# RWKV scan: chunk inverse in seven products instead of ten, key products in the other array corners, two VectorE operations moved to GpSimd

## The chip, the cores and the metric

One Trainium2 chip, one core. The metric is device time in microseconds (us) of one execution of the whole program, the median of the runs shown.

## The reference, cut to what matters

The program is a two-part transformer stack. The change touches one stage, the RWKV-7 recurrence, which runs in both directions over 768 tokens (256 of context, 512 of sequence) for 16 heads of 64 channels:

```python
def _wkv_step(S, inp):
    r_t, w_t, k_t, v_t, a_t, b_t = inp
    sa = jnp.einsum('zbhvk,zbhk->zbhv', S, a_t)
    S = S * w_t[..., None, :] + sa[..., :, None] * b_t[..., None, :] + v_t[..., :, None] * k_t[..., None, :]
    return S, jnp.einsum('zbhvk,zbhk->zbhv', S, r_t)
```

The kernel does it in chunks of 64 tokens. Inside a chunk the `sa` rows depend on each other through a strictly triangular 64x64 matrix, so that each chunk needs the inverse R of (1 - that matrix).

## The kernel before, in words

`rwkv_scan` (L3537) treats one head at a time, 12 chunks a head, in 3 groups (NG) of 4 chunks. The forward direction lies on partitions 0 to 63 (`lo`), the backward one on 64 to 127 (`hi`). So each product is two 64x64x64 matmuls, one per direction; `mmul` (L3957) issues both, each in the corner of the array whose rows and output partitions are the same half (lo to lo, hi to hi). `to_rows` (L3966), which adds rows of the result y, sends for odd chunks lo rows to hi partitions and hi rows to lo partitions.

The work of a head h is software-pipelined over three heads. `body` of TensorE (from L4026 on) has, interleaved by hand:

- for head h the *pair products* (`pair_set`, L4056: bh and kh against at_rt; 4 chunks 64 wide, 8 chunks 128 wide) and the *turns* (`turn`, L4068: bh and kh times a diagonal, 64 wide, 11 chunks); VectorE masks the pairs (`mask`, L3869), scales them (`scale`, L3881), makes R of the first level (`add_eye`) and its transpose T;
- for head h the *inverse*: five doubling levels (LEVELS = 5) of 3 groups, NZ = 15 steps, each of two products: `grow_z` (off x T, L4099), copied to Z by ScalarE (`copy_z`, L3792), and Z x R, added to R by VectorE (L3941), which then transposes R to T again (L3895). GpSimd makes the 15 masked `off` tiles (L3708) and the first R (L3703);
- for head h-1 the *walk*: 12 chunks j, each a chain of three parts, `walk_state` (X), `walk_solve` (SA = R X) and `walk_share` (state Sm). ScalarE copies X, SA and Sm out of PSUM (L3727, L3731, L3736), and the next part's matmul waits for that copy. The parts of chunks 0 to 2 and the first of chunk 3 lie among pair products and turns; the other 26 lie one by one in the 30 slots of the inverse (WALK_PARTS, L3545);
- for head h+1 the *factors*, spread over the same slots: five 128x768 activations on ScalarE, 14 operations on VectorE (`factor_part`, L3824), three on GpSimd (`factors`, L3682: km, kh, eed).

Every engine works through its own list in order, so a wait holds all that stands behind it. In VectorE's list, after `add_eye`, stand `add_bonus` (L3911), `split_block` (L3926: w_lo = w_raw - w_hi, 128x512) and `add_shift` (L3920: the bias, 128x256); the inverse's additions come after these. The DMA queue (SP) stores w_hi and w_lo once w_lo is made, loads the next block once the bias is added, and then loads factors and v of later heads.

The walk of the last head (15) runs in the next stage, `walk_finish` (L4188), beside the output projection.

## Time and profile before

| | |
|---|---|
| median of 3 runs | 4038.56 us (4037.82 to 4040.61) |
| span of the profiled execution | 4039.7 us, from its first to its last instruction |
| the scan in it | from 2812.16 us (first pair product of head 0) to about 3399 us |
| mean granted TensorE clock | 0.970 of full speed |

The profiled execution is known by its span alone; it lies 1.1 us over the median of the runs, inside their spread. A PE row is a matmul: each fp32 product of one direction is two records, so one `mmul` is x4. A row `x2` or `x4` merges records that follow each other. The duration of a PE row is from issue to the end of its results; what a product costs in a dense stretch is the step from one row's start to the next. PEclk is the granted clock (1.00 is 2.4 GHz, 0.50 is 1.2 GHz). A row of busy time by stretch gives start and end, length, then busy time and count of PE, PEld (weight loads), DVE (VectorE), ACT (ScalarE) and POOL (GpSimd), PEclk, the DMA share and GB/s. In square brackets at a row's end stands the idle time before it and what ended it.

### The profile page before, as it was taken

To read this page: it belongs to the slowest core of one execution; us is meant where nothing else is said; L and a number is where in the kernel's file an instruction comes from. 1 tells how busy PE (TensorE), PEld (TensorE's weight loads), DVE (VectorE), ACT (ScalarE), POOL (GpSimd) and SP (SyncE) were. 2 spreads that over 40 slices of the span, in tenths; PEclk is the share of its full clock that TensorE was granted. 3 is DMA by queue.
4 is the path that set the end of the run, shared out by engine and by line. 5 is a ranking of instruction groups with operands and counts; after the bars stand their busy time and mean duration, and the time that the engine had idled before them with its cause. 6 is when DMAs were issued, how large, how long until landed. Compare 5 with 4: busy or idle time off the path is not lost. (4 is left out here: it accounts for less than half of the span.)

```text
span 4039.7 us, 81581 instructions
## 1 busy us (share of the span) xinstructions
PE 3727.0 (92%) x32706; PEld 2683.2 (66%) x32706; DVE 2360.8 (58%) x3864; ACT 1204.0 (30%) x2668; POOL 1321.7 (33%) x1020
## 2 busy tenths in 40 slices
PE   8888999898999999899999997998999999899887
PEld 6667878657787898777344444874999998733333
DVE  4568882545985445565444445767888776623333
ACT  3352222344222322331111112224455454111112
POOL 4443444434445364573000000431555453000000
PEclk9999999999999999999999999999999999899999
DMA  4114542303554122345999995356333234589997
GB/s 128 56 53 170 184 157 93 104 1 105 178 187 146 66 96 75 99 138 228 404 420 420 420 420 212 134 177 201 88 89 91 78 93 147 199 366 422 421 421 316
DMA packets 231204, 787.80 MB, mean 195 GB/s; under 512 B 56008, under 2 KB 64024, under 8 KB 171136
## 3 DMA queue, kind: packets, MB, share of 16 engines
q1 hardware_dynamic: 225008, 764.12, 50.9%
q0 software_dynamic: 5328, 19.40, 1.2%
q8 instruction: 219, 3.59, 0.4%
q14 instruction: 73, 0.60, 0.0%
q10 hardware_dynamic: 576, 0.09, 0.0%
HBM read 736.15 MB, written 47.38 MB: 194 GB/s over the span
## 5 line engine op out<-in xcount | busy, mean ns | idle before, releaser
L2887 POOL DMA_INDIRECT moe0e_xg<-moe_h,moe_first_rows x20 | 18.9, 947 | 546.3 <-DVE moe_first_rows L3044 540.5
L3011 ACT ACT_TABLE_LOAD x32 | 41.1, 1283 | 519.2 <-PE moe1e_p_u L2957 262.4
L373 POOL TENSOR_TENSOR gmi_w_lo<-gmi_rows_w,gmi_w_hi 128x512 fp32r<-128x512 f32 x64 | 120.2, 1878 | 159.8 <-ACT gmi_w_hi L415 159.8
L3960 PE MATMUL scan_bank<-scan_T,scan_off 64*64 64x64 f32 x3840 | 159.4, 220 | 8.5 <-issue 5.7
L373 POOL TENSOR_TENSOR p_w_lo<-p_rows_w,p_w_hi 128x512 fp32r<-128x512 f32 (+3 forms) x88 | 113.5, 1291 | 159.9 <-ACT p_w_hi L415 159.9
L2887 POOL DMA_INDIRECT moe1e_xg<-moe_h,moe_first_rows x17 | 16.0, 940 | 451.0 <-DVE moe_first_rows L3044 444.4
L1159 POOL TENSOR_TENSOR f0u_w_lo<-f0u_w,f0u_w_hi 128x1024 fp32r<-128x1024 f32 x42 | 115.0, 2757 | 137.6 <-ACT f0u_w_hi L1175 137.6
L1159 POOL TENSOR_TENSOR f1u_w_lo<-f1u_w,f1u_w_hi 128x1024 fp32r<-128x1024 f32 x42 | 114.3, 2742 | 137.5 <-ACT f1u_w_hi L1175 137.5
L1227 DVE SCALAR_TENSOR_TENSOR f0u_ada<-hT,condition,f0u_ada 128x512 f32<-128x512 f32 x168 | 148.2, 949 | 16.4 <-DMA hT<-in_ada_w_dram 15.9
L1227 DVE SCALAR_TENSOR_TENSOR f1u_ada<-hT,condition,f1u_ada 128x512 f32<-128x512 f32 x168 | 140.5, 903 | 20.5 <-DMA hT<-in_ada_w_dram 20.0
L2984 PE MATMUL moe0e_p_y<-moe_ring,moe0e_gatedT 128*64 128x512 f32 x608 | 137.6, 605 | 7.8 <-ACT moe0e_gatedT L3013 7.8
L3960 PEld LDWEIGHTS scan_bank<-scan_T,scan_off 64*64 64x64 f32 x3840 | 137.2, 135 | 10.5 <-issue 6.8
L373 POOL TENSOR_TENSOR rp_w_lo<-rp_rows_w,rp_w_hi 128x512 fp32r<-128x512 f32 x48 | 79.9, 1666 | 164.8 <-ACT rp_w_hi L415 164.8
L2984 PE MATMUL moe1e_p_y<-moe_ring,moe1e_gatedT 128*64 128x512 f32 x512 | 113.4, 595 | 10.8 <-DVE x L3040 9.4
L3797 ACT ACTIVATE scan_Z<-scan_bank 128x256 f32<-128x256 f32 x240 | 91.4, 381 | 97.1 <-PE scan_bank L3960 95.8
L3960 PE MATMUL scan_bank<-walk_memory 64*64 64x64 f32 x1708 | 116.0, 222 | 4.3 <-issue 1.7
L2957 PE MATMUL moe0e_p_g<-gm_uT,moe0e_xT 128*64 128x512 f32 x444 | 118.1, 600 | 0.8 <-ACT moe0e_xT L3005 0.8
L2957 PE MATMUL moe0e_p_u<-gm_uT,moe0e_xT 128*64 128x512 f32 x444 | 116.2, 592 | 0.0
L440 DVE CAST gmi_x_hi<-hT 128x768 fp32r<-128x768 f32 x64 | 42.9, 670 | 125.2 <-PE gmi_bank L362 124.9
L2984 PEld LDWEIGHTS moe0e_p_y<-moe_ring,moe0e_gatedT 128*64 128x64 f32 x608 | 50.0, 139 | 86.8 <-issue 71.3
L3708 POOL TENSOR_TENSOR scan_off<-scan_pairs,scan_join 128x256 f32<-128x256 f32 x120 | 101.3, 880 | 0.0
L3708 POOL TENSOR_TENSOR scan_off<-walk_memory,scan_join 128x256 f32<-128x256 f32 x120 | 100.4, 873 | 0.0
(903 smaller groups left out, 11529.7 us busy)
## 6 DMA issues: line engine op xcount, KB each, us to landing
moe_ring<-in_moe_w_down_dram SPq DMA_DIRECT2D x140, 1024.0 KB, 18.0
gm_uT<-in_moe_w_gu_dram SPq DMA_DIRECT2D x111, 1024.0 KB, 16.6
moe_ring<-in_moe_w_gu_dram SPq DMA_DIRECT2D x102, 1024.0 KB, 24.7
walk_memory<-in_moe_w_gu_dram SPq DMA_DIRECT2D x60, 1024.0 KB, 24.4
hT<-in_ada_w_dram SPq DMA_DIRECT2D x48, 1024.0 KB, 6.8
f0u_w<-in_ffn_w_gate_up_dram SPq DMA_DIRECT2D x22, 1024.0 KB, 4.8
f1u_w<-in_ffn_w_gate_up_dram SPq DMA_DIRECT2D x22, 1024.0 KB, 4.8
gmi_rows_w<-in_ga_w_in_dram SPq DMA_DIRECT2D x64, 256.0 KB, 2.7
```

Of the source, the lines that this page charges most:

```text
L373: nc.gpsimd.tensor_tensor(w_lo[t % 2][:, 0:width], w[t % RAW][:, 0:width], w_hi[t % 2][:, 0:width], ALU.subtract).then_inc(w_lo_made, 1)
L440: nc.vector.tensor_copy(x_hi[t % 2][:, tok], hT[:, k, tok]).then_inc(x_hi_made, 1)
L1159: nc.gpsimd.tensor_tensor(w_lo[u][:, g], w[:, g], w_hi[u][:, g], ALU.subtract).then_inc(lo_made, 1)
L1227: ins = V.scalar_tensor_tensor(out=acc[:, z, :], in0=src, scalar=cond[:, n * HALF + k, z:z + 1], in1=acc[:, z, :], op0=ALU.mult, op1=ALU.add)
L2887: pool.indirect_dma_start(xg[:], None, H.h, bass.IndirectOffsetOnAxis(rows[:, 0:1], 0)).then_inc(gathered, 16)
L2957: mm = nc.tensor.matmul(p[r, :], xT[:, kd, r], weights(s, half, second)[:, k, g * HID:(g + 1) * HID], start=(kd == 0), stop=(kd == KD - 1) ...
L2984: mm = nc.tensor.matmul(p_y[n][r, :], aT[:, kh, r], ring[s, half][:, k, n * BANK:(n + 1) * BANK], start=(kh == 0), stop=(kh == KH - 1), sk ...
L3011: nc.scalar.activation(sg[:], p_g[:], ACT.Silu).then_inc(silu_ready, 1)
L3708: nc.gpsimd.tensor_tensor(off[n][:], strict(u, g), over4(join[:, l + 1, :]), ALU.mult).then_inc(s["off_ready"], 1)
L3797: A(Z[n % 2][:], quad(z_bank[n % 2]), ACT.Copy).then_inc(s["z_copied"], 1)
L3960: mm = nc.tensor.matmul(out[r], lhsT[r], rhs[r], start=start, stop=stop, skip_group_check=True)
```

## The change

The inverse takes 7 products per group instead of 10: with blocks of 32 (BLOCK_BITS) W is the part of the matrix inside the blocks beyond the first level; a first product gives the power (FIRST), three products Z x [power, R] of 128 columns square the power and extend R at once (stages 1 to 3), one adds the last power, and two (OUTER, FINAL) join the two blocks of 32. They are issued in 30 UNITS, the 9 squaring products in two halves. ScalarE copies the power (`copy_power`), VectorE adds and transposes. All products with kh (pairs, turns) and those of the walk with v use the other two corners of the array (`crossed`: hi rows to lo partitions and the reverse); v is loaded with its halves swapped, and pairs of b and of k get PSUM banks and masks of their own. The products with v move ahead of the part that needs them. `split_block` and `add_shift` go from VectorE's list to GpSimd's, right behind the masks. In `walk_finish` the walk gets the same order.

```diff
-LEVELS = 5
+BLOCK_BITS = 5
+PRODUCTS = 7
...
-                    for z, rows in ((0, lo), (1, hi)):
+                    for z, rows in ((0, hi), (1, lo)):
...
+                def split_block(h):
+                    pool.wait_ge(s["hi_made"], h + 1)
+                    nc.gpsimd.tensor_tensor(w_lo[:], w_raw[:], w_hi[:], ALU.subtract).then_inc(s["lo_made"], 1)
+
+                def add_shift(h):
+                    hs = slice(h * HK, h * HK + HK)
+                    pool.wait_ge(s["bonus_done"], h + 1)
...
                 def body(h, walk, ahead):
                     u = h % 2
+                    if h:
+                        pool.wait_ge(s["r_added"], h * ADDED)
                     for g in range(NG):
...
-                    for n in range(NZ):
-                        l, g = n // NG, n % NG
-                        if h:
-                            pool.wait_ge(s["z_ready"], (h - 1) * NZ + n + 1)
-                        nc.gpsimd.tensor_tensor(off[n][:], strict(u, g), over4(join[:, l + 1, :]), ALU.mult).then_inc(s["off_ready"], 1)
+                        nc.gpsimd.tensor_tensor(WR[:, g4, 1, :], strict(u, g), over4(join[:, 0, :]), ALU.mult).then_inc(s["r_joined"], 1)
+                        nc.gpsimd.tensor_tensor(off[:, g4, :], strict(u, g), over4(join[:, 1, :]), ALU.mult).then_inc(s["off_ready"], 1)
+                    for g in range(NG):
+                        nc.gpsimd.tensor_tensor(off_outer[:, 4 * g:4 * g + 4, :], strict(u, g), over4(join[:, 2, :]), ALU.mult).then_inc(s["outer_ready"], 1)
+                    split_block(h)
+                    add_shift(h)
                     if ahead is not None:
                         factors(ahead)
...
+                    copy_turned(0)
+                    early_walk(walk_sm, 1)
...
                     copy_turned(1)
+                    early_walk(walk_x, 2)
+                    early_walk(walk_sa, 2)
                     copy_turned(2)
+                    early_walk(walk_sm, 2)
+                    early_walk(walk_x, NG)
...
+                    def copy_power(n):
+                        act.wait_ge(s["r_added"], h * ADDED + adds_through(n))
+                        A(WR[:, chunks(n), 0, :], both(n)[:, :, 0, :], ACT.Copy).then_inc(s["z_copied"], 1)
+
+                    for k, (n, (first, end)) in enumerate(UNITS):
+                        if n // NG in (FIRST, OUTER):
+                            copy_z(n)
+                        walk_part(walk, k - 1)
+                        if squares(n) and end == 4:
+                            copy_power(n)
+                        if ahead is not None and k % 2 == 0 and k:
+                            factor_part(ahead, k // 2 - 1)
...
-                    mask(0)
+                    mask_b(0)
                     scale(0)
-                    mask(1)
-                    mask(2)
+                    mask_k(0)
+                    mask_b(1)
                     scale(1)
-                    mask(3)
-                    mask(4)
+                    add_eye(0)
+                    mask_b(2)
                     scale(2)
-                    add_eye(0)
+                    mask_k(1)
                     add_eye(1)
+                    mask_k(2)
                     add_eye(2)
...
+                def crossed(out, lhsT, rhs, start=True, stop=True):
+
+                    for r, o in ((hi, lo), (lo, hi)):
+                        mm = nc.tensor.matmul(out[o], lhsT[r], rhs[r], start=start, stop=stop, skip_group_check=True)
                     return mm
...
                     def turn(g):
...
+                        if g == 1:
+                            pe.wait_ge(s["kpairs_masked"], h * NG + 2)
+                            pe.wait_ge(s["bpairs_masked"], h * NG + 3)
...
+                            j, o = 4 * g + q, slice(q * CH, (q + 1) * CH)
+                            mm_b = mmul(banks[:, TURN_BANKS[g], o][:, 0, :], bh[:, j, :], eed[h % 3][:, j, :])
+                            mm_k = crossed(banks[:, TURN_BANKS[g], o][:, 1, :], kh[:, j, :], eed[h % 3][:, j, :])
...
+                            if stage == FIRST:
+                                mm = mmul(one(n)[:, q, :], off[:, j, :], T[:, j, :])
+                            elif squares(n):
+                                mm = mmul(both(n)[:, q], Z[:, j, :], WR[:, j])
+                            elif stage == OUTER:
+                                mm = mmul(one(n)[:, q, :], off_outer[:, j, :], T[:, j, :])
+                            else:
+                                mm = mmul(one(n)[:, q, :], Z[:, j, :], WR[:, j, 1, :])
...
+                    for k, (n, (first, end)) in enumerate(UNITS):
+                        product(n, first, end)
+                        walk_part(k - 1)
```

## Rows read from the trace of the kernel before

**Rows 1.** Busy time by stretch: head 0, heads 1 to 14, head 15.
```profile
2812.16:2847.34 35.18, 30.00 (x752) 28.71 (x754) 29.56 (x63) 12.14 (x24) 21.34 (x22) 0.87 0.48 126
2847.34:3364.48 517.14, 496.11 (x15519) 478.02 (x15516) 417.03 (x841) 267.87 (x840) 280.31 (x294) 1.00 0.31 83
3364.48:3399.27 34.79, 33.38 (x1059) 32.44 (x1054) 22.89 (x47) 15.57 (x56) 13.96 (x18) 1.00 0.11 31
```
**Rows 2.** The same for head 5: up to its first inverse product, and from there on.
```profile
2995.77:3005.98 10.21, 10.21 (x295) 10.18 (x293) 8.44 (x17) 4.12 (x13) 4.95 (x7) 1.00 0.21 42
3005.98:3032.59 26.61, 25.25 (x827) 23.99 (x824) 21.47 (x44) 15.10 (x48) 15.06 (x15) 1.00 0.36 104
```
**Rows 3.** PE in order of time, head 5: 128-wide pairs; first and fifth turn.
```profile
2997.04 0.41 PE L3960 MATMUL scan_bank<-scan_at_rt,scan_kh 64*64 64x128 f32 x4
2997.26 0.41 PE L3960 MATMUL scan_bank<-scan_at_rt,scan_bh 64*64 64x128 f32 x4
...
3002.88 0.31 PE L3975 MATMUL scan_bank<-scan_eed,scan_kh 64*64 64x64 f32 x4
...
3003.35 0.31 PE L3975 MATMUL scan_bank<-scan_eed,scan_kh 64*64 64x64 f32 x4
```
**Rows 4.** PE in order of time, head 5: solve of an odd chunk with its `to_rows`.
```profile
3011.82 0.27 PE L3960 MATMUL scan_bank<-walk_memory,scan_R 64*64 64x64 f32 x2
3011.84 0.27 PE L3969 MATMUL scan_bank<-walk_memory,scan_at_rt 64*64 64x64 f32 x2
...
3011.99 0.27 PE L3960 MATMUL scan_bank<-scan_T,scan_off 64*64 64x64 f32 x2
```
**Rows 5.** The same for the next, even chunk.
```profile
3015.08 0.33 PE L3960 MATMUL scan_bank<-walk_memory,scan_R 64*64 64x64 f32 x4 [0.18 <-ACT walk_memory L3727]
3015.24 0.49 PE L3969 MATMUL scan_bank<-walk_memory,scan_at_rt 64*64 64x64 f32 x4
3015.47 0.38 PE L3969 MATMUL scan_bank<-scan_v,scan_pairs 64*64 64x64 f32 x4
```
**Rows 6.** VectorE by line and shape, heads 1 to 14: busy us, mean ns.
```profile
L3895 DVE STREAM_TRANSPOSE scan_T<-scan_R 128x256 f32<-128x256 f32 x105 | 46.8, 445 | 3.6
...
L3941 DVE TENSOR_TENSOR scan_R<-scan_R,scan_bank 128x256 f32<-128x256 f32 x107 | 44.5, 416 | 33.7 <-PE scan_bank L3960 32.2
...
L3878 DVE TENSOR_TENSOR scan_pairs<-scan_bank,scan_masks 128x512 f32<-128x512 f32 x28 | 19.3, 690 | 5.1 <-PE scan_bank L3960 5.1
```
**Rows 7.** VectorE in order of time, head 5: bonus, weight split, bias.
```profile
3005.11 1.79 DVE L3917 TENSOR_TENSOR rw_y_bonus<-walk_memory,scan_bonus 64x256 f32<-64x256 f32 x2
3006.93 1.10 DVE L3928 TENSOR_TENSOR scan_w_lo<-scan_w_raw,scan_w_hi 128x512 fp32r<-128x512 f32 x1
3007.96 0.95 DVE L3923 TENSOR_TENSOR rw_y_bonus<-rw_y_bonus,scan_shift 128x256 f32<-128x256 f32 x1
```
**Rows 8.** ScalarE by line and shape, heads 1 to 14: copies of turned keys.
```profile
L3774 ACT ACTIVATE walk_memory<-scan_bank 128x512 f32<-128x512 f32 x14 | 8.4, 598 | 6.1 <-PE scan_bank L3975 6.1
```
**Rows 9.** ScalarE in order of time, head 5: walk copies, a factor.
```profile
3010.34 0.22 ACT L3736 ACTIVATE walk_memory<-scan_bank 128x64 f32<-128x64 f32 x1 [0.43 <-PE scan_bank L3960]
3010.46 0.93 ACT L3749 ACTIVATE scan_sq<-head_memory,head_cols 128x768 f32<-128x768 f32 x1
...
3011.55 0.22 ACT L3727 ACTIVATE walk_memory<-scan_bank 128x64 f32<-128x64 f32 x1
3012.20 0.31 ACT L3731 ACTIVATE walk_memory<-scan_bank,scan_w 128x64 f32<-128x64 f32 x1 [0.43 <-PE scan_bank L3960]
```
**Rows 10.** GpSimd in order of time, head 5: the fifteen masks.
```profile
3003.29 12.67 POOL L3708 TENSOR_TENSOR scan_off<-walk_memory,scan_join 128x256 f32<-128x256 f32 x15
```
**Rows 11.** The page's costliest groups: a weight split on GpSimd, in another stage.
```profile
L373 POOL TENSOR_TENSOR gmi_w_lo<-gmi_rows_w,gmi_w_hi 128x512 fp32r<-128x512 f32 x64 | 120.2, 1878 | 159.8 <-ACT gmi_w_hi L415 159.8
```
**Rows 12.** Busy time by stretch: two successive short stretches of head 0.
```profile
2824.50:2827.90 3.40, 1.17 (x41) 1.03 (x36) 3.33 (x6) 2.11 (x4) 3.40 (x5) 1.00 0.25 91
2827.90:2831.30 3.40, 3.26 (x62) 3.29 (x63) 2.77 (x7) 1.70 (x4) 3.40 (x5) 0.51 0.55 153
```

More of the change, by code:

```diff
@@ L3539, in rwkv_scan @@
     NG = STEPS // 4
-    NZ = LEVELS * NG
+    NI = PRODUCTS * NG
+    ADDED, COPIED, TURNED = 5 * NG, 5 * NG, 6 * NG
+    FIRST, LAST_POWER, OUTER, FINAL = 0, 4, 5, 6
+    UNITS = [(n, part) for n in range(NI) for part in ((0, 4),) * (n // NG not in (1, 2, 3)) + ((0, 2), (2, 4)) * (n // NG in (1, 2, 3))]
+    TURNS_BEFORE = (2, 3, 2, 3)
+    INV_BANK = (2, 1, 3, 0)
     lat = SEQ // CH
@@ L4008, in walk_share @@
+                    if 0 < j < STEPS - 1:
+                        mmul(ds_psum, eed[w % 3][:, j, :], Sm[:], start=False, stop=False)
+                    if i >= 0:
+                        to_rows(i, rt(w, j), Sm[:]).then_inc(s["yr_done"], 1)
                 def walk_share(w, j):
                     u = w % 2
+                    i = j - CSTEPS
+                    if i >= 0:
+                        pe.wait_ge(s["yr_done"], w * lat + i + 1)
                     pe.wait_ge(s["sa_copied"], w * STEPS + j + 1)
@@ L4061, in pair_set @@
                         wide = kinds * CH
[L4062 removed]
+                        for q in range(4):
+                            j, o = 4 * g + q, slice(q * wide, (q + 1) * wide)
                             rhs = at_rt[h % 3][:, 0:kinds, j, :]
[L4064 to L4066 removed]
+                            mm_b = mmul(bank[BPAIR_BANK[g]][:, o], bh[:, j, :], rhs)
+                            mm_k = crossed(bank[KPAIR_BANK[g]][:, o], kh[:, j, :], rhs)
@@ L4129, in _ @@
+                    for k, (n, (first, end)) in enumerate(UNITS):
+                        product(n, first, end)
+                        walk_part(k - 1)
+                        if k == 0:
+                            pe.wait_ge(s["bon_read"], h + 1)
+                        if ahead is not None and k % 2 == 0 and k:
+                            factor_part(ahead, k // 2 - 1)
                 keep_clock(nc, S, bank[7][:, 0:P], 13)
@@ L4148, in rwkv_tables @@
     incl = halves(early | same, early.T | same)
+    strict_of_values, incl_of_values = halves(early.T, early), halves(early.T | same, early | same)
     joins = []
-    for l in range(LEVELS + 1):
+    for l in range(BLOCK_BITS + 1):
         m = 1 << l
@@ L4323, in walk_share @@
                     if j < STEPS - 1:
-                        mmul(ds_psum, walk.bkT[:, j, 0, :], walk.SA[:], start=False).then_inc(ds_ready, 1)
+                        values_to_x(j + 1).then_inc(xv_done, 1)
+                        if i >= -1:
+                            values_to_rows(i + 1, walk.pairs[:, j + 1, 3, :], walk.v[:, j + 1, :], start=i == -1).then_inc(yv_done, 1)
                 def turn_o(t, h):
```

376 lines of the change are left out of this document (196 added, 180 removed).

## The prediction

> **What bounds the kernel now.** I first read busy time by stretch, to see which engine fills the scan. In heads 1 to 14, PE is busy 496 of 517 us at a granted clock of 1.00, 36.94 us a head, while VectorE, the next, is busy 417 us, 29.8 a head [rows 1]. Head 0, which has no walk, is filled by VectorE instead (29.56 of 35.18). In one head, the part before the inverse is solid PE (10.21 of 10.21 us), the rest nearly so (25.25 of 26.61) [rows 2]. So in 15 of 16 heads TensorE's list is the bound. The next question is what a product costs there. In a dense stretch four 64-wide `mmul` take 0.47 us, 0.117 each, and a 128-wide one starts 0.22 after the one before [rows 3].
>
> Then I looked for products in the other corners. `to_rows` of an odd chunk is the only such work beside straight products. There R X and rt Sm start 0.02 us apart, and the next product, 0.17 after the first, finds both issued [rows 4]. For the even chunk, where both use the same corners, the second starts 0.16 after the first and the third 0.23 later: 0.39 for what took 0.17 [rows 5]. So a crossed product beside a straight one is nearly free, for 64 columns at least.
>
> **The change, part by part**, per head. *TensorE's inverse.* Now 30 products of 4 chunks: 120 x 0.117 = 14.0 us. After: 12 products 64 wide, 48 x 0.117 = 5.6, and nine 128 wide, 36 x 0.22 = 7.9: 13.5. That alone gains 0.5.
>
> *Crossed products.* Pairs cost 8 x 0.117 + 16 x 0.22 = 4.5 and turns 22 x 0.117 = 2.6; with every second one beside its neighbour, half: 3.5 gained. In the walk 12 products of v into X and 11 into the state, 23 x 0.117 = 2.7, come to lie beside others. Rows show no 128-wide crossed pair: its gain lies between nothing (as in-line) and all of it; I take all, since the nearest row, rows 4, overlapped fully. Together 6.7 us of PE work go, and 36.9 - 6.7 = 30.2 would be left if TensorE still decided. It will not.
>
> One rule speaks against this. The Trainium skill, "TensorE: Matmul & The Clock Gate" (Part 3), says that a weight load runs beside matmuls in flight only when its row group differs; a crossed product has the row group of a straight one, so by it k would line up behind b. In rows 4 the trace disagrees; by the rule the sum would be that of the rival "no overlap" below.
>
> *What replaces it before the inverse.* I laid out the new lists from the first pair product, T = 0. VectorE's last addition ends at 0.57. A 256-wide mask costs 0.42, like the addition of that shape, a 512-wide one 0.69, a transpose 0.445, scaling and adding the unit 0.42 each [rows 6]. In the new order mask b0 ends at 1.2, k0 2.05, b1 2.8, scale 3.2, the first unit and transpose 4.1, b2 4.8, scale 5.3, k1 6.0, k2 7.6, the last transpose 8.5, the bonus (1.79 [rows 7]) 10.4. TensorE's `turn(1)` has a new wait, for mask k1: it stands from about 4.7 to 6.05, with the walk's chunk 2 queued behind it. ScalarE then copies the turned keys (0.60 [rows 8], about 0.5 for the last group) ahead of X and Sm of chunk 2. That chain (X 7.7, SA 8.4, Sm 9.2) lets the first inverse product go at 9.4 instead of 10.2.
>
> *The 30 units.* 26 walk parts lie among them, one chain. From X's copy to SA's takes 0.65 us at least, ScalarE idle 0.43 of it [rows 9]; SA's copy is 0.09 longer, so the mean link is 0.68. TensorE's work per link is a unit of 0.44 to 0.47, 5.5 straight products per chunk / 3 x 0.117 = 0.21, and 0.05 to restart after a wait (0.16 against 0.117 [rows 5]): 0.73. I take 0.75; 25 links are 18.75. Five factor operations on ScalarE stand in the chain: now Sm to X with one of them and a copy of Z took 1.21 [rows 9], 0.56 over a link; 5 x 0.56 = 2.8. Near the end each product needs its transpose, which VectorE makes only behind the next addition: 2 x 0.42 + 0.445 + 0.3 after a product's end, against a link of 0.75; I count 0.9 for the two places. With 0.5 for the first unit and 0.6 for the last, 0.5 + 18.75 + 2.8 + 0.9 + 0.6 = 23.6. A head takes 9.4 + 23.6 = 33.0, bounds 30.2 (TensorE) and 36.94 (as now): **3.9 less**.
>
> *VectorE.* It loses split and bias (1.10 + 0.95 [rows 7]), gains 3 transposes (1.34) and 0.15 of masks: 29.8 becomes 29.2 of 33.0 us. That is tight, but no bound yet.
>
> *Split and bias on GpSimd.* The split takes 1.88 there [rows 11]; the bias I bound by 0.95 and 1.9. Fifteen masks, 12.67 us [rows 10], become six, and the first R masks stay three: they end near 9.6, the split 11.5, the bias (waiting for the bonus, 10.4) near 12.5 to 13.4. Queued behind are `factors`: km, kh and eed; km started after the old masks, 20.2 us into the head [rows 10], and waits for ScalarE's third factor, near 14. On SP the two stores of the split and the load that waits for the bias go out about where they did (3008.03 and 3008.91 ended, 12.3 and 13.1 into the head [rows 7]); stores and load have the 20 us to the next head's first use. So I cost both at nothing; if that cover were gone, 1.88 + 0.95 = 2.8 a head.
>
> *The sum.* Heads 1 to 14: 14 x 3.9 = 54.6. Head 15 has no factors: 34.79 [rows 1] to 33.0 - 2.8 = 30.2, 4.6. Head 0 is VectorE's: between 0 and 4, I take 2. The last walk keeps its chain: 0, between -1.5 and +1.5. In all 61. The profiled span, 4039.7, is 1.1 over the median, 4038.56; taken from the median: **3978 us**.
>
> **The rivals.** *Better:* links at 0.68 and no loss at the late transposes: 25 x 0.07 + 0.9 = 2.65 a head, 37 in all, 3941. For it: ScalarE's repeated 0.43 idle [rows 9]; against: VectorE at 88%.
>
> *The clock falls.* In head 0 it went to 0.51 after 3.40 us in which PE was busy 1.17 [rows 12]. The wait in `turn(1)` makes such a thin stretch in each head (by my list about 2 of 3.4 us busy). At half clock the 1.3 us of products that follow it (turns, bonus) take twice as long: 14 x 1.3 = 18, so 3996.
>
> *No overlap:* only the 0.5 of the inverse and the gain of heads 0 and 15 at most shrunk likewise: 4038.6 - 15 x 0.5 = 4031. Rows 4 speak against it.
>
> *Slower: the copy of the power holds the walk.* ScalarE's `copy_power` waits for VectorE's addition and stands in front of the next walk copy. VectorE's work apart from masks, scaling, unit, bonus, split, bias, 15 additions and 12 transposes is 29.8 - 22.8 = 7.0 us of factors. If an operation of these stands in front of each of the nine squaring additions (0.77 on average), the walk gets up to 0.77 later nine times. It decides from 3.9 / 9 = 0.43 on; at 0.6 a head gets 5.4 - 3.9 = 1.5 longer: 4038.6 + 21 - 6.6 = 4053. At 0.43 exactly, heads 0 and 15 alone gain: 4032. For it: VectorE's share; against: two links (1.5) hold addition, transpose and 0.63 us more.
>
> **How the numbers follow.** Forecast 0.48 (3978, its own range 3960 to 4000), better 0.14, clock 0.12, no overlap 0.06, the deciding point (4032) 0.07, slower 0.13. A measurement here can tell about 0.2%, 8 us. Faster by more: 0.48 + 0.14 + 0.12 and two thirds of no overlap, 0.78; within: 0.09; slower: 0.13. The range leaves out the slower case and the far tails: 3938 to 4033.
>
> **What would show it.** Right: first pair to first inverse product 9 to 9.8 us, with TensorE idle for VectorE's mask in front of `turn(1)`; pairs of b and k 128 wide starting together, 0.22 per two; heads of 32 to 34 us; PE busy under 85%; the split ending on GpSimd before km without km waiting. Wrong: b and k 0.22 apart each (no overlap); PEclk under 1.00 in heads 1 to 14; ScalarE waiting for VectorE's addition more than 0.4 us per squaring product, or heads over 36 us.

## The result, and the profile after

The changed kernel takes **4068.61 us** (median of 4 runs, 4064.59 to 4069.89), the kernel before 4039.59 beside it: a ratio of 1.0062, with a 95% interval of 1.0049 to 1.0076. The forecast was 3978, the range 3938 to 4033. The change makes the program slower, by 25 us by the ratio and 29 by the medians.

In the profiled execution (span 4067.7) the loss is all in the middle heads. Busy time by stretch, as in [rows 1] and [rows 2]: head 0, heads 1 to 14, head 15 up to its last inverse product, and head 5 in two parts.

```profile
2809.23:2841.02 31.79, 26.66 (x607) 24.04 (x611) 28.14 (x64) 12.03 (x24) 15.40 (x15) 0.84 0.52 140
2841.02:3388.94 547.92, 465.85 (x13510) 422.39 (x13504) 395.89 (x869) 272.08 (x840) 196.66 (x196) 0.93 0.28 78
3388.94:3423.87 34.93, 31.34 (x922) 28.75 (x914) 21.48 (x48) 15.53 (x56) 8.92 (x11) 0.90 0.11 30
...
2994.51:3004.89 10.38, 7.26 (x299) 6.65 (x291) 9.05 (x19) 4.32 (x14) 7.20 (x10) 1.00 0.21 41
3004.89:3032.56 27.67, 24.26 (x685) 21.62 (x682) 19.36 (x44) 15.18 (x47) 6.86 (x5) 1.00 0.33 100
```

Heads 1 to 14 take 547.92 / 14 = 39.14 us instead of 36.94; 14 x 2.2 = 30.8. Head 0 gains 3.4, head 15 loses 1.1 (its last product came 33.83 us into it before). Together +28.5, against 28.0 more of span. TensorE is busy less (465.85 for 496.11), VectorE too (395.89 for 417.03), and yet each head is longer: no engine fills a head now, and the granted clock of the stretch is 0.93, where it was 1.00.

Two things in TensorE's list of head 5, in order of time (columns: start, length, engine, operation; idle time in brackets): products of b and k 128 wide that start together, and a stop in the middle of the first turns.

```profile
2996.17 0.28 PE L4021 MATMUL scan_bank<-scan_at_rt,scan_kh 64*64 64x128 f32 x2
2996.18 0.31 PE L4006 MATMUL scan_bank<-scan_at_rt,scan_bh 64*64 64x128 f32 x2
2996.28 0.28 PE L4021 MATMUL scan_bank<-scan_at_rt,scan_kh 64*64 64x128 f32 x2
2996.29 0.31 PE L4006 MATMUL scan_bank<-scan_at_rt,scan_bh 64*64 64x128 f32 x2
...
2997.99 0.31 PE L4006 MATMUL scan_bank<-scan_eed,scan_bh 64*64 64x64 f32 x4
2999.89 0.27 PE L4021 MATMUL scan_bank<-scan_eed,scan_kh 64*64 64x64 f32 x2 [1.59 <-issue]
```

The first four rows are one chunk: 0.11 us per pass, 0.22 for b and k, where one of them alone took that long [rows 3]. So the overlap that the forecast stood on is complete. The last row is what it did not see. Between two products of one group, with no semaphore between them, TensorE has nothing to do for 1.59 us ("issue": it waits for nothing that the profile names). One packet of kind "instruction" lies in front of it, from 2997.15 to 2998.26.

I counted such **stalls** in heads 1 to 14: two weight loads over 0.3 us apart, the second waiting for no semaphore. The changed kernel has 40 of them, 40.4 us; the kernel before 20, 18.1 us. In front of the inverse it is 26.6 us against 1.0. Of those over 0.5 us (33) the median ends 1.4 us after an instruction packet has ended, 2.5 after it began. The waits of heads 1 to 14 (engine, line, what it waited for: us, times, longest) show them among the "issue" rows, and two more that the prediction named. Not all of the row of weight loads (PEld) is stalls: 114 of its 138 loads, 53.5 us, do wait for a semaphore, whose release the profile did not find; the stalls above leave these out.

```profile
POOL scan_km L3716 <- ACT scan_t L3783: 98.6, 14, 9.3
PEld scan_bank L4006 <- issue: 74.4, 138, 2.2
ACT scan_WR L3829 <- DVE scan_WR L3939: 21.1, 33, 1.2
PE scan_bank L4006 <- issue: 18.3, 21, 2.2
PE scan_bank L4021 <- issue: 9.2, 12, 1.6
PE scan_bank L4015 <- issue: 1.9, 3, 1.3
```

And the **clock**: it stands at half (1.2 GHz) for 78.5 us of heads 1 to 14, in 11 of the 14; before, never. Head 2 in three successive stretches: a stall, what follows it, and the fall.

```profile
2882.90:2884.78 1.88, 0.27 (x20) 0.14 (x11) 1.84 (x4) 0.02 (x1) 1.52 (x3) 1.00 0.00 0
2884.78:2887.36 2.58, 2.38 (x96) 2.20 (x95) 2.51 (x7) 2.06 (x6) 2.22 (x4) 1.00 0.02 6
2887.36:2894.19 6.83, 5.86 (x128) 5.51 (x130) 4.25 (x8) 2.56 (x11) 3.96 (x5) 0.50 0.35 115
```

Of the 15 falls in heads 1 to 14, 8 come 6 to 10 us into a head, in 5 heads 0.5 to 2.6 us after a stall, as here, and in 3 (10, 11 and 13) 0.1 to 2.4 us after TensorE waited 0.4 to 1.4 us for VectorE's mask in front of `turn(1)`. 7 more, the late falls, come 23 to 27 us into a head, 1.5 to 2.4 us after the last of three waits of TensorE (0.4 to 0.6, 0.4 and 0.8 us) beside ScalarE's factor operations. Five heads have stalls in front of the inverse and no early fall, and three a wait in front of `turn(1)` of 0.9 to 1.7 us and none, so neither always brings one.

### The profile page after: what moved, and what is told of

The parts are those of the page before. It is cut to its first block and busy times, and to the rows that moved or that the text cites. A ratio compares the mean times of both kernels' runs of the same rounds, so it can differ in the third digit from the quotient of the medians.

```text
span 4067.7 us, 76888 instructions
## 1 busy us (share of the span) xinstructions
PE 3689.7 (91%) x30402; PEld 2618.3 (64%) x30402; DVE 2336.0 (57%) x3896; ACT 1208.1 (30%) x2668; POOL 1224.1 (30%) x908
## 5 line engine op out<-in xcount | busy, mean ns | idle before, releaser
L4006 PE MATMUL scan_bank<-scan_WR,scan_Z 64*64 64x128 f32 (+1 forms) x3840 | 251.7, 261 | 8.9 <-DVE scan_Z L3931 4.3
L4006 PEld LDWEIGHTS scan_bank<-scan_WR,scan_Z 64*64 64x64 f32 x3840 | 196.0, 141 | 14.4 <-DVE scan_Z L3931 8.1
L3939 DVE TENSOR_TENSOR scan_WR<-scan_WR,scan_bank 128x256 f32<-128x256 f32 x144 | 59.9, 416 | 85.4 <-PE scan_bank L4006 84.7
L4006 PE MATMUL scan_bank<-walk_memory 64*64 64x64 f32 x1064 | 86.8, 239 | 17.6 <-ACT walk_memory L3766 8.1
L2177 POOL TENSOR_TENSOR gmo_w_lo<-gmo_w,gmo_w_hi 128x512 fp32r<-128x512 f32 x64 | 96.4, 1525 | 8.5 <-ACT gmo_w_hi L2313 8.5
L415 ACT ACTIVATE gmi_w_hi<-gmi_rows_w 128x512 fp32r<-128x512 f32 x64 | 40.4, 632 | 195.7 <-PE gmi_bank L362 193.9
```

Source lines behind the costliest of these rows:

```text
L415: nc.scalar.activation(w_hi[t % 2][:, 0:width], w[t % RAW][:, 0:width], ACT.Copy).then_inc(w_hi_made, 1)
L2177: nc.gpsimd.tensor_tensor(w_lo[s % RING][:, half[h]], raw[(2 * s + h) % RAW][:], w_hi[s % RING][:, half[h]], ALU.subtract).then_inc(w_lo_m ...
L3939: V.tensor_tensor(WR[:, g4, 1, :], WR[:, g4, 1, :], both(n)[:, :, 1, :], ALU.add).then_inc(s["r_added"], 1)
L4006: mm = nc.tensor.matmul(out[r], lhsT[r], rhs[r], start=start, stop=stop, skip_group_check=True)
```

## The experiments

All runs but e4_filled and i1_serial, which stand in the text, in one table; the columns from "head" on are heads 1 to 14 of the profiled execution, means in us (stalls and half clock: sums). "Front" is the first pair product to the first inverse product, "units" the rest of a head. The ratio is to the kernel before on the same chip. A profiled execution is one of several: it lay 9.7 us under the median of its runs in g1_at_later, 8.6 in e1_straight, 5.3 in g3_both, and 4.5 over it in h1_straight_order, so means of heads carry an uncertainty of up to 0.7 us, and the ratios decide.

| run | ratio (95%) | head | front | units | stalls | half clock |
|---|---|---|---|---|---|---|
| before | 1 | 36.94 | 10.29 | 26.65 | 18.1 | 0 |
| changed | 1.0062 (1.0049, 1.0076) | 39.14 | 10.62 | 28.52 | 40.4 | 78.5 |
| e1_straight | 1.0052 (1.0035, 1.0069) | 38.27 | 11.22 | 27.05 | 5.0 | 6.8 |
| e2_k_behind_b | 1.0060 (1.0038, 1.0082) | 38.97 | 10.80 | 28.17 | 40.7 | 34.1 |
| e3_split_on_vector | 1.0077 (1.0048, 1.0107) | 39.12 | 10.55 | 28.57 | 42.7 | 68.3 |
| g1_at_later | 1.0050 (1.0032, 1.0069) | 38.11 | 10.55 | 27.56 | 42.5 | 51.2 |
| g2_norm_split | 1.0031 (1.0019, 1.0044) | 37.84 | 10.68 | 27.16 | 43.5 | 78.5 |
| g3_both | 1.0016 (1.0002, 1.0030) | 37.24 | 10.67 | 26.57 | 41.3 | 71.7 |
| g4_straight_both | 0.9990 (0.9980, 1.0000) | 36.45 | 11.19 | 25.26 | 6.4 | 0 |
| h1_straight_order | 0.9967 (0.9955, 0.9980) | 35.98 | 10.91 | 25.07 | 2.5 | 0 |
| h2_crossed_order | 0.9992 (0.9982, 1.0001) | 37.02 | 10.14 | 26.88 | 51.6 | 47.8 |
| h3_crossed_ten | 1.0106 (1.0089, 1.0123) | 40.30 | 10.45 | 29.85 | 73.9 | 85.3 |
| h4_before_split_gpsimd | 1.0044 (1.0031, 1.0057) | 38.30 | 10.51 | 27.79 | 33.1 | 10.1 |
| i2_fill64 | 1.0079 (1.0062, 1.0096) | 39.62 | 10.63 | 28.99 | 53.3 | 71.7 |
| i3_serial_again | 1.0114 (1.0061, 1.0166) | 39.44 | 13.78 | 25.65 | 11.1 | 10.2 |

### The two halves of the change

**e1_straight**: seven products alone. v, the value products and the products of k go back to straight corners, and the value products of y to their old place behind `walk_solve`'s own.

```diff
-                    for r, o in ((hi, lo), (lo, hi)):
+                    for r, o in ((lo, lo), (hi, hi)):
...
-                    for z, rows in ((0, hi), (1, lo)):
+                    for z, rows in ((0, lo), (1, hi)):
...
-                            values_to_rows(i + 1, pairs[u][:, j + 1, 3, :], vs[u][:, j + 1, :], start=i == -1).then_inc(s["yv_done"], 1)
...
+                        to_rows(i, pairs[w % 2][:, j, 3, :], vs[w % 2][:, j, :])
```

> The seven-product inverse and the work in GpSimd's queue stay; the k products, the value products of the walk and the loads of v go back to straight corners, so that no product of k runs beside one of b. Theory A (TensorE's instructions come too slowly for four corners at once; each such stall of 1 to 2.4 us also lets the clock fall in the first 10 us of a head): stalls of TensorE over 0.3 us that end without a semaphore fall from 40 us in heads 1 to 14 to under 20 us, the clock falls in the first 10 us of a head (9 of 14 heads after the change) are gone or nearly so, TensorE's busy time rises by 4 to 6 us per head, and the time is 4020 to 4050 us. Theory B (the crossed overlap is all gain, and the loss is in the walk's chain and the new waits between ScalarE and VectorE): the head gets longer by the 3 to 6 us that the overlap saved, and the time is 4110 to 4160 us.

It took 4065.40 us. Busy time of its heads 1 to 14, and all the "issue" waits of matmuls in them:

```profile
2839.32:3375.17 535.85, 494.17 (x13503) 464.86 (x13501) 389.34 (x869) 271.99 (x840) 196.29 (x196) 0.99 0.29 80
```

```profile
PE scan_bank L4015 <- issue: 3.3, 3, 1.6
PE scan_bank L4006 <- issue: 0.3, 1, 0.3
```

Theory A is right on the stalls (40.4 to 5.0) and on the clock (78.5 to 6.8), wrong on the time (4020 to 4050 expected): crossing costs and gains about the same. TensorE's busy time rises by 2.0 us per head, not by the 4 to 6 expected. And a third thing stands out that neither theory had: without stalls, with the clock at 1.00, the units still take 26.62 or 26.63 us in 9 of 14 heads. The forecast had 23.6.

**h3_crossed_ten**: the other half alone. Crossed products as changed; the inverse, its copies, additions and masks taken over from the kernel before, on banks 0 to 3; split and bias on VectorE.

```diff
-                    for k, (n, (first, end)) in enumerate(UNITS):
-                        product(n, first, end)
+                    for n in range(NZ):
+                        g = n % NG
+                        if n + 1 < NZ:
+                            grow_z(n + 1)
```

> The other half of the change by itself: crossed products, banks, masks, order and walk as changed, but the inverse in ten products on GpSimd's fifteen masks, and the split and the bias on VectorE, as in the kernel before. The prediction's step (6.2 us of TensorE per head go, nothing comes in their place): heads of 32 to 34 us, 3985 to 4010 us. Theory A2: stalls of 35 to 45 us and half clock in heads 1 to 14; heads of 35.5 to 37.5 us, 4025 to 4050 us.

It took 4085.14 us, worse than theory A2's bound: 73.9 us of stalls, 44.4 of them in the units, whose ten products leave TensorE little idle time. Its heads 1 to 14:

```profile
2839.60:3403.80 564.20, 476.81 (x15526) 447.20 (x15518) 407.43 (x854) 266.03 (x840) 272.05 (x294) 0.92 0.28 76
```

### What the stalls hang on

**e2_k_behind_b**: in each group of pairs and turns first the products of b, then those of k.

```diff
                         for q in range(4):
                             j, o = 4 * g + q, slice(q * wide, (q + 1) * wide)
-                            rhs = at_rt[h % 3][:, 0:kinds, j, :]
-                            mm_b = mmul(bank[BPAIR_BANK[g]][:, o], bh[:, j, :], rhs)
-                            mm_k = crossed(bank[KPAIR_BANK[g]][:, o], kh[:, j, :], rhs)
+                            mm_b = mmul(bank[BPAIR_BANK[g]][:, o], bh[:, j, :], at_rt[h % 3][:, 0:kinds, j, :])
+                        for q in range(4):
+                            j, o = 4 * g + q, slice(q * wide, (q + 1) * wide)
+                            mm_k = crossed(bank[KPAIR_BANK[g]][:, o], kh[:, j, :], at_rt[h % 3][:, 0:kinds, j, :])
```

> The changed kernel, but each group of pairs and each group of turns issues its products of b first and its products of k behind them, in place of b and k in turn; the corners, the banks and all else stay. Theory A: at half the rate of instructions TensorE's stalls without a semaphore fall to under 20 us in heads 1 to 14 and the early clock falls mostly go; the products of the pairs and turns take about 3 us longer per head, of which stalls and half clock give back 3 to 5: 4030 to 4075 us. Theory B: nothing is given back, about 3 us per head are lost: 4105 to 4125 us.

4067.24 us, stalls 40.7: the expectation failed on the stalls. The order in the list does not keep b and k apart; k's first product starts at 2995.46, before b's last one, behind which it stands in the list, starts (2995.63) and ends (2995.85). TensorE in order of time, head 5, first group of pairs:

```profile
2995.14 0.54 PE L4006 MATMUL scan_bank<-scan_at_rt,scan_bh 64*64 64x64 f32 x10
2995.46 0.27 PE L4021 MATMUL scan_bank<-scan_at_rt,scan_kh 64*64 64x64 f32 x2
...
2995.63 0.22 PE L4006 MATMUL scan_bank<-scan_at_rt,scan_bh 64*64 64x64 f32 x1
```

**i1_serial** and **i3_serial_again** therefore put a wait between them, on the kernel of h2_crossed_order (below); the turns get the same.

```diff
+                        mm_b.then_inc(s["bpairs_ready"], 1)
+                        pe.wait_ge(s["bpairs_ready"], h * NG + g + 1)
                         for q in range(4):
                             j, o = 4 * g + q, slice(q * wide, (q + 1) * wide)
                             mm_k = crossed(bank[KPAIR_BANK[g]][:, o], kh[:, j, :], at_rt[h % 3][:, 0:kinds, j, :])
...
                         mm_k.then_inc(s["kpairs_ready"], 1)
+                        pe.wait_ge(s["kpairs_ready"], h * NG + g + 1)
```

> The crossed kernel of h2_crossed_order, with each group of pairs and of turns in order: its products of b, a wait of TensorE for the last of them, its products of k, a wait for the last of those. Corners, banks and instructions stay; only b and k never run at once. Theory A2 (feeding all four corners at once is what outruns the instructions, not the crossed corners as such): stalls in front of the inverse fall from 32.5 us in heads 1 to 14 to under 6 us, half clock from 48 to under 15 us; the part in front of the inverse takes 10.8 us as with straight corners plus 0.2 to 0.3 for each of 12 waits, 13 to 14.5 us; 4050 to 4085 us. Rival (crossed products stall wherever they stand): stalls there stay over 20 us.

> The same kernel as i1_serial, for a profile at the usual clock (that of i1_serial was taken at a mean granted clock of 0.74 throughout and shows 1.6 us of stalls in front of the inverse, but at a lower rate of products). Theory A2: stalls in front of the inverse under 6 us and half clock under 15 us in heads 1 to 14 at the usual clock too, 11.5 to 14 us in front of the inverse, 4070 to 4090 us. Rival: stalls there over 20 us.

The first has a ratio of 1.0092 (1.0075 to 1.0109), the second takes 4083.99 us. The "issue" waits of matmuls in heads 1 to 14 of the second:

```profile
PE scan_bank L4006 <- issue: 6.1, 15, 0.7
PE scan_bank L4021 <- issue: 0.3, 1, 0.3
```

In front of the inverse 1.3 us of stalls are left of 32.5. So crossed corners do not stall by themselves there. Over the traces, the stalls in front of the inverse go by how fast TensorE takes its instructions. Records of products and weight loads there (567 to 576 a head), divided by the time less the stalls, and the stalls in 14 heads:

| kernel | records per us | stalls there, us |
|---|---|---|
| i3_serial_again | 41.7 | 1.3 |
| e1_straight | 50.7 | 0.6 |
| h1_straight_order | 52.3 | 0.7 |
| h4_before_split_gpsimd | 55.9 | 2.7 |
| before | 56.4 | 1.0 |
| e2_k_behind_b | 60.8 | 19.7 |
| g3_both | 64.9 | 26.1 |
| changed | 65.5 | 26.6 |
| h2_crossed_order | 72.9 | 32.5 |

Up to 56 a us there are 2.7 us at most, from 61 on they grow with the rate; the other crossed kernels lie at 65 to 69 with 26.5 to 30.9 us. The changed kernel and e1_straight fetch 107 packets of 16 KB each in heads 1 to 14; a stall over 0.5 us follows 33 of them in the first and 4 in the second. That the rate is the cause is the reading of this table and of the packets, and it is not shown: every kernel above 60 also feeds straight and crossed corners at once, and no run changed the supply of instructions by itself. In the units the mean rate does not order the kernels: 49 records per us go with 13.8 us of stalls in the changed kernel, 51 with 4.4 in e1_straight, 54 with 9.8 in i3_serial_again, 64 with 17.1 in the kernel before.

### What makes the units long

Two places stood out in the order of time of ScalarE, VectorE, GpSimd and TensorE, units 8 to 12 of head 5 of the changed kernel:

```profile
3012.90 1.81 POOL L3716 TENSOR_TENSOR scan_km<-head_memory,scan_t 128x768 f32<-128x768 f32 x1 [5.93 <-ACT scan_t L3783]
3013.01 2.11 DVE L3869 SCALAR_TENSOR_TENSOR walk_memory<-head_memory,scan_negkk,scan_e_exc 128x384 f32<-128x384 f32 x1
3015.05 0.41 DVE L3939 TENSOR_TENSOR scan_WR<-scan_WR,scan_bank 128x256 f32<-128x256 f32 x1
3015.49 0.38 ACT L3829 ACTIVATE scan_WR<-scan_bank 128x256 f32<-128x256 f32 x1 [0.52 <-DVE scan_WR L3939]
3015.77 0.93 ACT L3789 ACTIVATE scan_e_inc<-head_memory,head_sides 128x768 f32<-128x768 f32 x1
3016.60 0.21 ACT L3766 ACTIVATE walk_memory<-scan_bank 128x64 f32<-128x64 f32 x1
...
3017.09 1.54 PE L4006 MATMUL scan_bank<-ones,scan_sq 64*64 64x1 f32 x48
...
3019.28 0.31 ACT L3761 ACTIVATE walk_memory<-scan_bank,scan_w 128x64 f32<-128x64 f32 x1 [1.31 <-PE scan_bank L4006]
```

First a chain: VectorE's factor operation on at_rt takes 2.11 us beside GpSimd's km, and ends 0.41 us after km does; behind it the addition; ScalarE's copy of the power waits 0.52 for that; e_inc and the walk's copy of Sm stand behind the copy. Then the 24 products for the key norms, 1.54 us in one piece, in front of the part that SA needs: ScalarE idle for 1.31.

**g1_at_later** moves the at_rt operations, **g2_norm_split** cuts the norms, **g3_both** has both, **g4_straight_both** has both on the kernel of e1_straight.

```diff
-                    if at in (8, 10):
-                        o = half[at // 2 - 4]
+                    if at in (17, 19):
+                        o = half[at // 2 - 8]
...
+                SS_PARTS = {9: (0, 3), 10: (3, 7), 12: (7, 12)}
...
                         product(n, first, end)
+                        if ahead is not None and k in SS_PARTS:
+                            norm_part(ahead, *SS_PARTS[k])
                         walk_part(k - 1)
```

> The changed kernel, with VectorE's two factor operations on at_rt (128x384, 2.12 and 1.47 us while GpSimd makes km and kh beside them, in front of the first squaring additions) moved from units 8 and 10 to units 17 and 19. Theory D (ScalarE's copy of the power waits there for VectorE's late addition, 0.61 and 0.70 us, and the next walk copy stands behind it): the units get 0.8 to 1.3 us shorter per head, 4050 to 4060 us. Rival (the link is set by TensorE or by the factor operations of ScalarE in the same place): 4064 to 4072 us.

> The changed kernel, with the 24 products of one column for the key norms, which stand in one piece of 1.38 us between two parts of the walk in unit 12, cut into three pieces of 3, 4 and 5 chunks (0.35, 0.46 and 0.58 us) right in front of the walk parts of units 9, 10 and 12, where TensorE waits 0.4, 0.6 and 1.1 us for ScalarE. Theory E (the piece stands whole in the walk's chain; the prediction's 23.6 us for the units did not count it): units 0.9 to 1.4 us shorter per head, 4048 to 4057 us, and the clock falls 23 to 27 us into a head are gone or rarer. Rival (the chain waits elsewhere for as long): 4064 to 4072 us.

> The edits of the two runs before together, on the changed kernel with its crossed products. D and E both right, terms adding: units 1.7 to 2.7 us shorter, heads of 36.3 to 37.4 us, 4030 to 4044 us. Stalls of TensorE without a semaphore stay near 40 us in heads 1 to 14. Rival (stalls and half clock take up what the chain gives): over 4055 us.

> The same two edits on the kernel with straight corners (seven products, no k product beside one of b). TensorE's own work, 35.3 us per head, is now the bound: heads of 36.0 to 36.6 us instead of 38.3, no half clock in heads 1 to 14, stalls under 10 us: 4030 to 4042 us. If D and E are wrong: 4060 to 4068 us as without them.

4062.56, 4053.14, 4050.05 and 4037.56 us. In the profiled executions the units of the first three get shorter by 0.96, 1.36 and 1.95 us per head, those of g4 by 1.79 against e1_straight. By the ratios the three gain less, 0.35, 0.9 and 1.3 us per head. The norms (g2) and both edits together are clear of noise; the part of at_rt alone is not (the intervals of g1 and the changed kernel overlap, and those of g3 and g2), and g1's time missed the 4050 to 4060 expected. g1's at_rt operations, away from km and kh, take a third of the 1792 ns that they took on average (columns: busy us, mean ns):

```profile
L3885 DVE SCALAR_TENSOR_TENSOR scan_at_rt<-head_memory,scan_negkk,scan_e_exc 128x384 f32<-128x384 f32 x18 | 10.9, 608 | 0.0
```

g3's gain (1.0062 to 1.0016) falls short of the 4030 to 4044 us expected; stalls and half clock stay, though the late falls are gone. In g4, where TensorE is busy 482.79 of 510.36 us, half clock is gone and 6.4 us of stalls are left:

```profile
2844.39:3354.75 510.36, 482.79 (x13503) 462.19 (x13500) 358.45 (x869) 269.73 (x840) 194.80 (x196) 1.00 0.31 83
```

**h1_straight_order** and **h2_crossed_order** add to g4 and g3 a new order in front of the inverse.

```diff
-                    add_eye(0)
                     mask_b(2)
-                    scale(2)
                     mask_k(1)
+                    scale(2)
+                    add_eye(0)
                     add_eye(1)
...
-                    copy_turned(2)
                     early_walk(walk_sm, 2)
+                    copy_turned(2)
```

> The kernel with straight corners, seven products, the at_rt operations later and the key norms in three pieces (the last run of the set before), and the list in front of the inverse reordered: VectorE masks k1 right behind b2, ahead of the first unit additions, and ScalarE copies the third group of turned keys behind Sm of chunk 2. Theory F (the two waits of TensorE in front of the inverse, 0.62 us for mask k1 and 0.79 us for Sm, are what makes 11.15 us there out of 10.2): 10.0 to 10.5 us there, heads 35.0 to 35.8 us, 4020 to 4030 us, faster than the kernel before by 0.3 to 0.5 per cent. Rival (the unit additions come later and the first inverse product waits for their transposes instead): 4034 to 4042 us as before this edit.

> The same four edits on the changed kernel with its crossed products. Without stalls and half clock its heads would take 34 us by the shortest ones. Theory A2 (a stretch in which all four corners are fed uses some 120 instructions per us where a straight one uses some 73, and the next block of instructions comes too late; what crossed products gain in front of the inverse is lost there): stalls without a semaphore stay at 35 to 45 us in heads 1 to 14, half clock at 40 to 80 us, time 4035 to 4050 us, slower than the same kernel with straight corners by 8 to 20 us. Rival (stalls come from the order around turn 1 and go with it): stalls under 20 us, 4000 to 4020 us.

h1 took 4028.70 us against 4042.29: a ratio of 0.9967 (0.9955 to 0.9980), **the only version here whose interval lies wholly below 1**, and some 1% faster than the changed one. The front is only 0.28 us shorter (10.91), for 1.4 us of waits, and heads of 35.98 us are over the 35.0 to 35.8 expected, so theory F holds for a part. h2 took 4040.29: its shortest head passes that part in 8.11 us, the mean in 10.14, and its stalls (51.6) are the most of all kernels of seven products but for the filled ones. Busy time of heads 1 to 14 of h1 and its largest "issue" wait of matmuls, then the same of h2:

```profile
2850.20:3353.85 503.65, 483.33 (x13503) 462.31 (x13501) 356.00 (x869) 268.40 (x840) 194.71 (x196) 1.00 0.31 84
```

```profile
PE scan_bank L4006 <- issue: 1.6, 2, 1.1
```

```profile
2843.96:3362.25 518.29, 452.02 (x13510) 412.92 (x13506) 361.11 (x869) 269.02 (x840) 194.76 (x196) 0.95 0.30 82
```

```profile
PE scan_bank L4006 <- issue: 23.0, 30, 2.2
```

### The clock by itself

**e4_filled** and **i2_fill64** put extra products, whose results nobody reads, where TensorE waits in the units: 17 of 512 columns (1 in most of units 1 to 11, 2 in units 6, 8, 9 and 10, 3 in unit 11), and 23 of 64 columns.

```diff
+                    FILL = {4: 2, 6: 4, 9: 3, 10: 5, 12: 9}
...
                         product(n, first, end)
+                        if h:
+                            for _ in range(FILL.get(k, 0)):
+                                mmul(bank[4][:, CH:2 * CH], at_rt[h % 3][:, 0, 0, :], at_rt[h % 3][:, 0, 0, :])
                         walk_part(k - 1)
```

> The changed kernel with 1 to 3 extra products 512 columns wide, over both straight corners, into a bank nobody reads then, behind the products of units 1 to 11 of heads 1 to 15, where TensorE waits for ScalarE's copies. Theory C (the clock falls 23 to 27 us into a head come from TensorE's three waits of 0.6, 0.8 and 1.2 us beside ScalarE's factors): these falls (7 of 14 heads, 24 us at half clock) vanish, those in the first 10 us stay, and the time falls by 5 to 12 us to 4056 to 4064 us. Rival: the extra products stand in the walk's way and the chain costs as much as the clock gives back, 4068 to 4090 us.

> The changed kernel, with 23 extra products 64 wide per head (0.117 us each, 2.7 us) into a bank nobody reads then: 2, 4, 3, 5 and 9 of them in front of the walk parts of units 4, 6, 9, 10 and 12, where TensorE waits 0.25, 0.6, 0.5, 0.7 and 1.1 us for ScalarE. Theory C (the clock falls there because TensorE waits): the late falls (7 of 14 heads, 24 us of half clock) vanish, those in front of the inverse stay, units 0.3 to 0.6 us shorter per head, 4058 to 4066 us. Rival (late falls cost nothing, since the chain there runs on ScalarE and VectorE): 4066 to 4074 us, the falls gone all the same.

e4 took 4226.84 us, a ratio of 1.0440 (1.0411 to 1.0469): mis-sized, since a product 512 wide holds its corner for 0.86 us, 14.6 us a head. i2 took 4075.67. Of the seven late falls e4 has none and i2 one, as theory C has it, but i2's units are longer, not shorter (28.99 for 28.52): with 92 weight loads and 92 matmuls more per head came more stalls (in the units 22.4 us for 13.8). So what the falls cost by themselves stays untested. Worked out instead: over the 28 middle heads of the changed kernel and of e3_split_on_vector, a fit gives a head of 36.1 us, plus 0.28 per us at half clock, plus 0.53 per us of stall, with 0.45 left over. For the changed kernel that is 78.5 / 14 x 0.28 = 1.6 and 40.4 / 14 x 0.53 = 1.5 us per head.

### Split and bias

**e3_split_on_vector** puts them back on VectorE in the changed kernel; **h4_before_split_gpsimd** moves them, and nothing else, in the kernel before.

```diff
                     add_bonus()
+                    split_block()
+                    add_shift()
                     if ahead is not None:
                         fc = Chain(dve, s["factor_step"], ahead * FACTOR_STEPS)
```

```diff
                         nc.gpsimd.tensor_tensor(off[n][:], strict(u, g), over4(join[:, l + 1, :]), ALU.mult).then_inc(s["off_ready"], 1)
+                    split_block(h)
+                    add_shift(h)
                     if ahead is not None:
                         factors(ahead)
```

> The changed kernel with the weight split and the bias addition back in VectorE's list behind the bonus, as before the change; GpSimd goes from the masks straight to the factors. Prediction's step (it costs nothing on GpSimd, and takes 1.10 + 0.95 us per head from VectorE): VectorE's busy time rises from 28.3 to about 30.3 us per head, the first additions of the inverse come up to 2 us later in a head, time 4065 to 4100 us. Rival (GpSimd's additions hold up the factors, or slow VectorE while they run): faster than the changed kernel, 4040 to 4065 us.

> The kernel before with its weight split and bias addition moved to GpSimd's queue right behind the fifteen masks, nothing else. By the prediction TensorE bounds it, so two VectorE microseconds less per head change nothing: 4034 to 4044 us. Rival: behind fifteen masks instead of nine they push km and kh some 2 us later, to where the last factor operations of VectorE wait for them: 4045 to 4070 us.

e3: 4074.21 us, heads 39.12 for 39.14. No difference that can be told. VectorE's busy time does not rise to 30.3 us per head, as expected: it is 28.27 with both operations back on VectorE, 28.28 without them. They take 1.11 us there (1.10 + 0.95 in the kernel before [rows 7]), and the bonus, beside which GpSimd makes the split in the changed kernel, takes 1.31 us per head instead of 2.29. So on GpSimd they took no busy time from VectorE. Bonus, split and bias of head 5 on VectorE in e3, and the bonus of the changed kernel, during which GpSimd makes the split:

```profile
3006.46 1.35 DVE L3968 TENSOR_TENSOR rw_y_bonus<-walk_memory,scan_bonus 64x256 f32<-64x256 f32 x2
3007.85 0.69 DVE L3979 TENSOR_TENSOR scan_w_lo<-scan_w_raw,scan_w_hi 128x512 fp32r<-128x512 f32 x1
3008.46 0.42 DVE L3974 TENSOR_TENSOR rw_y_bonus<-rw_y_bonus,scan_shift 128x256 f32<-128x256 f32 x1
```

```profile
3003.83 2.33 DVE L3980 TENSOR_TENSOR rw_y_bonus<-walk_memory,scan_bonus 64x256 f32<-64x256 f32 x2
```

h4: 4062.77 us, slower, but not by the wait that the rival named. Behind fifteen masks the split ends 21 us into a head, and with it the stores and loads that wait for it move from 12 to 21 us into a head and later. The stretch from 22 to 32 us into head 5, the kernel before and h4; the last columns are clock, DMA share and GB/s:

```profile
3017.77:3027.77 10.00, 9.02 (x312) 8.70 (x310) 7.74 (x19) 3.54 (x13) 1.95 (x1) 1.00 0.38 105
```

```profile
3029.91:3039.91 10.00, 8.23 (x294) 7.98 (x292) 7.24 (x16) 3.44 (x13) 3.50 (x2) 1.00 0.71 198
```

DMA is nearly twice as busy there, and stalls in the units go from 17.1 to 30.3 us. Between 28 and 32 us into a head they go from 4.5 to 15.6 (14 heads), at a DMA share of 0.80 for 0.27; but between 32 and 36 us they go from 7.8 to 13.9 at a share of 0.18 for 0.21, and the median instruction packet takes no longer (1.0 us for 1.1). That crowding delays the instructions is a guess, not tried by itself.

## Why the prediction was wrong

**The step that failed is the sum of the units, "0.5 + 18.75 + 2.8 + 0.9 + 0.6 = 23.6".** They take 28.5 us. That is 4.9 of the 6.1 us that a head is over the forecast of 33.0; the other 1.2 lie in front of the inverse. The sum left out the key norms, which stand in the walk's chain: cutting them takes 1.36 us per head away in the profiled execution, 0.9 by the ratios. It called VectorE's 29.2 us "tight, but no bound yet", and what stands in front of the squaring additions in its list stood at nothing in the sum, and at 0.77 us an operation in a rival. Moving two operations takes 0.96 away in the profiled execution, 0.35 by the ratios (0.43 between g2 and g3), which is within the noise. The rival's 7.0 us of factors, from which the 0.77 comes, is a remainder; the rows of VectorE's factor operations before the change add up to 8.7 us a head. They also show that these two take nearly twice the 0.77 (busy us, mean ns):

```profile
L3837 DVE SCALAR_TENSOR_TENSOR scan_at_rt<-head_memory,scan_negkk,scan_e_exc 128x384 f32<-128x384 f32 x18 | 25.9, 1440 | 0.0
```

With straight corners and no stalls the units stand at 26.6, 3.0 over the sum; both edits bring 24.83 in the shortest head, and 1.2 of the 3.0 stay unplaced: their cause is open.

**Nothing stood in the sum for stalls and clock.** By the fit they are 1.5 and 1.6 us of the 6.1. Stalls were there to be read before the change (18.1 us); the prediction had no row for them and no rival. The clock it had as a rival alone. The Trainium skill, "Runtime: NRT & Kernel Launch" (Instruction fetch mechanics), says that an engine fetches its instructions in blocks of 16 KiB while it runs, and that the cost of crossing a block is mostly hidden. In front of the inverse the traces agree at 56 records per us (1.0 us of stalls in 14 heads), and not at 61 (19.7).

Point by point:

- *Crossed products run beside straight ones:* right, fully, at 128 columns too. The rule that the prediction weighed there (the Trainium skill, "TensorE: Matmul & The Clock Gate", Part 3) would have put k behind b; the trace disagrees again, with 0.22 us for both.
- *6.7 us of TensorE's work go:* at full clock, head 5 shows 31.52 busy for 35.46 [rows 2], 3.9. How much of the rest is only the way lone products are counted stays open.
- *9.4 us in front of the inverse:* 9.62 in the shortest head; 10.62 in the mean, with 1.9 of stalls. TensorE did stand in front of `turn(1)` for VectorE's mask, but in 8 of 14 heads, for 0.9 us on average where 1.35 was laid out; head 5 shows no such wait, as a stall of 1.59 us came first. The mechanism was right in part.
- *VectorE 29.2 us:* 28.3, near it, but not by the step given: taking split and bias away, counted as 2.05 us, made no difference to it (28.27 with both on VectorE, in e3). *Split and bias cost nothing:* right on the time; the bias ends 12.5 us into head 5 (forecast 12.5 to 13.4), and km waits for ScalarE's t (98.6 us in 14 heads), not for them.
- *Head 0, -2:* -3.4. *Head 15, -4.6:* +1.1; it has a stall of 2.28 us and 6.8 us of half clock.
- *The rival "the clock falls":* the fall came, and its price was near (1.3 forecast, 1.6 by the fit). That the price is near is chance: it was counted for every head from the wait in `turn(1)`, which stands before 3 of the 15 falls; before 5 stands a stall (e1_straight, with 5.0 us of stalls, has no early fall), before 7 the waits in the units. It came on top of the rest instead of alone.
- *The rival "the copy of the power holds the walk":* it waits 21.1 us in 14 heads, 0.17 per squaring product, far under the 0.43 from which it decides. Named rightly, but as a term of the sum it was real, and it stood at nothing there.
- *Range and chances:* 4068.6 lies outside 3938 to 4033. The rivals each changed one thing; what happened was three at once.

## What to carry to other kernels

When a bound engine is relieved, lay out the chain that takes over with every instruction of the queue in it, small ones too: here 24 one-column products and the place of two VectorE operations were worth 1.3 to 2 us of a 39 us head. Before raising the rate at which an engine takes instructions, look in its trace for idle time that no semaphore explains: here such rows stood there before the change (18.1 us), and what overlap gained came back as stalls and as a lower clock. The part of a change that a run can carry alone is worth running alone: seven products on straight corners, with the chain cleaned and the order in front changed, beat both kernels (by 0.3% and some 1%).

## What the hardware showed that was not expected

- TensorE stands still in the changed kernel without a semaphore to wait for, two weight loads up to 2.4 us apart, and goes on 1.4 us after an instruction packet of 16 KB has ended (median of 33 stalls). In front of the inverse that takes at most 2.7 us in 14 heads up to 56 records per us, and 32.5 at 73.
- Products of k that stand behind those of b in the list, in other corners, start 0.17 us before b's last one starts (e2_k_behind_b): order in the list does not keep corners apart; in i3_serial_again a wait for a semaphore did.
- VectorE's 128x384 operation on at_rt takes 0.61 us by itself and 2.11 beside GpSimd's 128x768 multiplication; the bonus takes 2.29 us a head beside GpSimd's split and 1.31 without it (changed, e3_split_on_vector).
- With two operations moved to GpSimd in the kernel before (h4_before_split_gpsimd), and no instruction of TensorE changed, TensorE's stalls in the units went from 17.1 to 30.3 us; DMA traffic moved to the same place, but that it is the cause is not shown.
